# A hybrid of two network blocks on one core: two heads in turn in the state-space loop, the rotary steps behind it, and other places for units of the first block

## The chip, the core and the metric

The kernel is one program on one core of a Trainium2 chip. The metric is the device time in microseconds of one execution, and the median of the runs is compared. Five engines run side by side, each through its own list of instructions: TensorE (PE) multiplies matrices into PSUM, VectorE (DVE) and ScalarE (ACT) read and write PSUM and SBUF, GpSimd (POOL) does some small work, and SyncE (SP) issues the transfers of weights. They wait for each other through semaphores.

## What is computed

256 tokens of width 1024 go through a first block (a mixer of two kinds of attention, and experts) and then twice through a second block (feed-forward, mixer, feed-forward). All of it is fp32.

```python
def first_block(x, ...):
    u = rmsnorm(h, norm_mix_g) @ w_in
    o_sb = stick_breaking(u[..., :1536])           # 8 heads of 64, softplus of the scores, suffix sums
    o_rw = rwkv7(u[..., 1536:])                    # 8 heads of 64: S_t = S_{t-1} diag(w_t) + (S_{t-1} (-kk_t)) (kk_t * a_t)^T + v_t k_t^T
    h = h + concat([o_sb, o_rw]) @ w_out
    return rmsnorm(h + experts(rmsnorm(h)))        # 32 experts, 2 of them weighted per token

# in rwkv7, the norms of the keys:
    kk = k * k_k
    kk = kk * rsqrt(max(sum(kk * kk, over a head), 1e-24))

def second_block(x, ...):
    for l in range(2):
        x = x + 0.5 * swiglu(rms_norm(x), ...)
        u = rms_norm(x) @ w_in[l]
        y_ssd  = ssd_mixer(...)     # state space, 16 heads of 64, both directions, chunks of 128
        y_mla  = mla_mixer(...)     # 8 heads, 64 + 32 rotary, softmax
        y_conv = conv_mixer(...)    # depthwise, 3 taps
        x = x + concat([y_ssd, y_mla, y_conv]) @ w_out[l]
        x = x + 0.5 * swiglu(rms_norm(x), ...)

def ssd_chunked(x, dt, a, bm, cm):  # one direction
    decay  = exp(where(lower, a_cs[l] - a_cs[s], -inf))
    cb     = einsum('lgn,sgn->lsg', cm, bm)
    y_diag = einsum('lsg,lsgr,sgrp->lgrp', cb, decay, x * dt)
    y_off  = cm @ (state of the chunk before) * exp(a_cs)
    return y_diag + y_off
```

## The kernel before

**Layout.** Activations stand as feature x token in tiles of 128 partitions x 256 tokens. The token dimension is two chunks of 128 (`tok(0)`, `tok(1)`), and a 64-wide head fills one half of the partitions, so a tile `f` holds two heads, 2f and 2f + 1. The working memory is one arena addressed; PSUM is eight banks `PS[0]` to `PS[7]` of 128 x 512 elements. `bank(b, mark)` on PE waits until the work that `mark` names has read bank b, and notes who will empty it next.

**fp32 products.** The projections and the feed-forward split each operand into a high part and a rest, and add three products (`mm3`). The weights come through a ring of five slots of 128 x 2048 elements. SP fills a slot when PE is through with the load five before (`spent`), ACT makes the high part (`rhi`, line 2260), DVE the rest (`rlo`, line 1486), and PE waits for both in `take(n)`. In SSD, in the attentions and in the key norms the operands are plain fp32 or exact constants and are multiplied once (`mm`).

**Order of work.** No planner stands between the source and the engines. Each engine has a function (tensor, vector, scalar, gpsimd, sync) in which its steps are called in the order in which it runs them, and semaphores join the engines: `hit` marks a step, `wait_ge` waits for one. Where a helper records an operation, all of its uses have one line: 538 a matmul, 541 a transpose, 1475 a scalar_tensor_tensor, 1478 a tensor_scalar, 2260 an activation.

**First block.** Its units are the rw projections j = 0 to 6 (PE), each with a weight pass of DVE (`ahead`) and DVE's shift mixing; the sums of squares of the keys and their spread over a head (`head_sums`, `head_spread`, `kk`; reciprocal in line 1565); `decays`, `inputs` and `kk_a` on DVE; the attention matrices of four groups g and their masks (line 1697 and the ones near it); the first level of a block inverse (`level_first`, with transposes, and the copy of line 1576); six projections `sb_proj(i)` in the banks of `sb_bank`; the bonus term (line 1708); and `inverse`, whose units u step through levels and groups, `level_y(u)` and `level_x(u)`, DVE's part being line 1611 and, for the last level, line 1613. Stick-breaking softplus, weights, values and sums are hung onto units u by number in the lists of PE, DVE and ACT.

**State-space loop.** For each k = 2h + d (head h, direction d) PE builds the exponent of the decay in bank k % 4 (`ssd_decay`), ACT takes its exponential into one of `NM` buffers `Md`, in two halves with their own bias, and DVE multiplies it by `cb` (line 2154). `ssd_values(h)` multiplies it with the inputs `xd`: four matmuls of 128 x 64 on 128 tokens, into the lower or upper 64 partitions of bank 4 + f % 4. For an odd head it then adds the far terms of both directions with two matmuls on the identity, and DVE adds the skip term (line 1475). Before the loop's values stand the states and `ssd_far`. `head_rope(1, step)` is DVE's share of the query and key norms and the rotation of the second half of the tokens, called from within this loop at k = 9, 17 and 25 (lines 2062 to 2079).

**Heads behind it.** `turn_heads(tt)` transposes queries and keys, `conv_tile` is a half tile of projection (24 matmuls) for the third mixer, and then for h = 0 to 8 a half tile, `scores(h + 1)`, `turned(h)` and `values(h - 1)` follow each other. DVE takes the maximum of the scores (line 2168), ACT the exponential, PE transposes it, DVE copies it out of PSUM (line 2175), PE multiplies it with the values. Between them ACT and DVE make the parts of the next weights, the first of them in `mixer_load`.

Of the kernel before, what the change touches and what calls it, by code (L numbers as in the profile page):

```python
# [170 lines left out]
def program(nc, I, out):  # L171

    MUL, ADD, SUB, MAX, EQ = ALU.mult, ALU.add, ALU.subtract, ALU.max, ALU.is_equal
    with ExitStack() as ctx:
# [215 lines left out]
        sb_bank = lambda i: (4, 6, 5, 7, 3, 2)[i]  # L390
# [64 lines left out]
        NM = 6  # L455
        Md = v3(B0 + 9264, NM)
# [64 lines left out]
        def tensor(e, w):  # L521
# [246 lines left out]
            def inverse():  # L768

                for u in range(4, NU + 2):  # L770
                    if u < NU:
                        level_y(u)
                    if u in (6, 7, 15, 16):
                        h = {6: 0, 7: 2, 15: 4, 16: 6}[u]
                        sb_weights(h)
                        sb_weights(h + 1)
# [3 lines left out]
                    if u in (18, 19):  # L780
                        sb_values(u - 16)
                    if 20 <= u < 26:
                        masked((u - 20) // 3, (u - 20) % 3)
                    if u == 21:
                        w.wait_ge("sb_sq")
                        head_sums(sq2, 3, "sb")
                    if u in (24, 26):
                        spread_half(3, "sb", u // 26, ("sb_m", u // 26 * 2 + 1))
# [131 lines left out]
            def first_block():  # L920
                w.dma(d_first, 32)
                norm(0)
                for j, f in enumerate(RW_F):
# [40 lines left out]
                sb_scores(1)  # L964
                sb_proj(5)
# [237 lines left out]
            def mixer(l):  # L1203
# [116 lines left out]
                def ssd_values(h):  # L1320
                    po, f, ob = 64 * (h % 2), h // 2, 4 + (h // 2) % 4
                    if po == 0:
                        bank(ob, ("yo", l, f))
                    for d in range(2):
                        w.wait_ge("md", l, 2 * h + d)
                        for c in range(2):
                            w.wait_ge("xd", l, 2 * c + 1)
                            p = mm(PS[ob][po:po + 64, tok(c)], xd[d][:, c, h * 64:h * 64 + 64], Md[:, (2 * h + d) % NM, tok(c)], d + c == 0, d + c == 2)
                    if po:
                        for d in range(2):  # L1330
                            w.wait_ge("far", l, d, f // 4)
                            p = mm(PS[ob][:, tok(1 - d)], y_far[d][:, 128 * f:128 * f + 128], C("ident"), False, d == 1)
                    p.then_inc(*w.hit("yv", l, h))
# [1646 lines left out]
```

## Time and profile before

| what | value |
|---|---|
| runs | 1900.99, 1900.48, 1890.29 us, median 1900.48 |
| profiled execution | 1892.44 us, its span 1890.7 us |
| PE, DVE, ACT busy | 1819.9, 1202.1, 941.8 us |
| state-space loop, layer 0 | 928.71 to 959.31 us |
| scores of head 0 to values of head 7, layer 0 | 971.50 to 1023.11 us |
| first block up to the inverse | 0 to 119.46 us |

The profile's page gives busy time by engine and a row for each group of instructions. The timeline lists what an engine does in the order of time: the start in us from the span's start, the duration of the group, the engine and line, what is written and read, partitions and shapes, the count, and in brackets the idle time ahead of it and who ended it. The profile records an fp32 matmul as two, so a count of 8 stands for four matmuls. Rows of PE overlap a little, since the matmuls are pipelined; from start to start is the safe way to read what a step costs.

### The profile page before, as it was taken

What the parts mean: (1) busy time and instruction counts of PE and PEld (TensorE: products, weight loads), DVE (VectorE), ACT (ScalarE), POOL (GpSimd) and SP (SyncE); (2) the same over time, 40 slices, a digit from 0 to 9 for tenths busy, and PEclk for the clock granted to TensorE, in tenths of its full rate; (3) what the DMA queues carried; (4) which work ended last, traced back from release to release, by engine and by line L of the source; (5) the groups of instructions that cost most, each with busy time, mean ns of one, the idle gap of its engine ahead of it and who ended that gap; (6) DMA issues with size and microseconds to landing.
All of it is one profiled execution on the core that took longest, in us unless ns stands there. A gap on an engine that the chain in (4) does not pass through costs nothing.

```text
span 1890.7 us, 26150 instructions
## 1 busy us (share of the span) xinstructions
PE 1819.9 (96%) x10830; PEld 1579.7 (84%) x10830; DVE 1202.1 (64%) x1510; ACT 941.8 (50%) x1231; POOL 104.3 (6%) x78
## 2 busy tenths in 40 slices
PE   7899989999999899989999999999998999999999
PEld 7888788888888788878898888888887988888887
DVE  5945568677777855448857655455555696756553
ACT  6444356455654644347554454444434666445442
POOL 1413011000000000000110000000000012000000
PEclk9999989999999999999999999999999999999999
DMA  8320146899999455545222465556654541245653
GB/s 275 113 71 1 34 157 223 303 343 333 338 333 324 142 178 189 190 134 178 90 68 91 155 200 179 192 168 197 190 189 145 168 134 35 100 157 182 193 180 111
DMA packets 191063, 329.93 MB, mean 175 GB/s; under 512 B 7776, under 2 KB 150496, under 8 KB 186592
## 3 DMA queue, kind: packets, MB, share of 16 engines
q1 hardware_dynamic: 190800, 327.74, 52.3%
q8 instruction: 85, 1.39, 0.3%
q0 software_dynamic: 144, 0.52, 0.1%
q14 instruction: 34, 0.28, 0.0%
HBM read 327.18 MB, written 1.05 MB: 174 GB/s over the span
## 4 chain that ended last, share of the span: by engine, by line
PE 78%; DVE 12%; ACT 4%; DMA 3%; issue 2%; POOL 1%; SPq 0%; DVEq 0%; ACTq 0%; POOLq 0%
PE ps L538 75%; DVE rlo L1486 3%; PE ps L541 3%; DVE arena L1475 2%; ACT rhi L2260 2%; DMA ring<-in_exp_w_up 2%; ACT arena L2260 1%; DMA ring<-in_w_in 1%; DVE xnl L1475 1%; DVE arena L1478 1%; DVE small L2168 0%; DVE xtok L1475 0%; POOL arena L2823 0%; DVE small L2055 0%; DVE arena L2198 0%
## 5 line engine op out<-in xcount | busy, mean ns | idle before, releaser
L1486 DVE TENSOR_TENSOR rlo<-ring,rhi 128x2048 fp32r<-128x2048 f32 x274 | 627.0, 2290 | 372.5 <-ACT rhi L2260 372.1
L2260 ACT ACTIVATE rhi<-ring 128x2048 fp32r<-128x2048 f32 x274 | 521.4, 1906 | 281.0 <-PE ps L538 134.2
L538 PE MATMUL ps<-rhi,xnh 128*128 128x512 f32 (+1 forms) x768 | 301.8, 393 | 0.8 <-DVE arena L1708 0.8
L538 PE MATMUL ps<-rhi,xnl 128*128 128x512 f32 (+1 forms) x768 | 296.4, 386 | 0.0
L538 PE MATMUL ps<-rlo,xnh 128*128 128x512 f32 (+1 forms) x768 | 296.0, 385 | 0.0
L538 PE MATMUL ps<-xnh,rhi 128*128 128x256 f32 (+2 forms) x824 | 242.9, 295 | 3.0 <-DVE xnl L1475 3.0
L538 PE MATMUL ps<-xnl,rhi 128*128 128x256 f32 (+2 forms) x824 | 236.6, 287 | 0.0
L538 PE MATMUL ps<-xnh,rlo 128*128 128x256 f32 (+2 forms) x824 | 236.4, 287 | 0.0
L538 PE MATMUL ps<-rhi,hhi 128*128 128x512 f32 x544 | 205.4, 395 | 0.0
L538 PE MATMUL ps<-rhi,xwr 128*128 128x512 f32 x528 | 180.5, 404 | 2.2 <-issue 1.9
L538 PE MATMUL ps<-arena 128*128 128x128 f32 (+10 forms) x1256 | 165.1, 297 | 16.3 <-DVE arena L2175 9.4
L2260 ACT ACTIVATE arena<-ps 128x512 f32<-128x512 f32 (+4 forms) x196 | 93.8, 497 | 163.2 <-PE ps L538 97.0
L538 PE MATMUL ps<-rhi,hlo 128*128 128x512 f32 x448 | 172.2, 390 | 2.2 <-DVE hlo L2228 2.2
L538 PEld LDWEIGHTS ps<-rhi,xnh 128*128 128x128 f32 x768 | 144.4, 188 | 31.1 <-DVE arena L1708 1.6
L538 PE MATMUL ps<-rlo,hhi 128*128 128x512 f32 x432 | 169.1, 391 | 0.0
L538 PEld LDWEIGHTS ps<-rhi,xnl 128*128 128x128 f32 x768 | 144.3, 188 | 29.5
L538 PEld LDWEIGHTS ps<-rlo,xnh 128*128 128x128 f32 x768 | 144.6, 188 | 27.7 <-issue 0.5
L538 PEld LDWEIGHTS ps<-xnh,rhi 128*128 128x128 f32 (+2 forms) x824 | 159.9, 194 | 6.7 <-issue 6.1
L538 PEld LDWEIGHTS ps<-arena 128*128 128x128 f32 (+3 forms) x1256 | 132.1, 175 | 36.5 <-DVE arena L2175 11.0
L538 PEld LDWEIGHTS ps<-xnl,rhi 128*128 128x128 f32 (+2 forms) x824 | 159.9, 194 | 1.3 <-issue 1.0
L538 PEld LDWEIGHTS ps<-xnh,rlo 128*128 128x128 f32 (+2 forms) x824 | 159.4, 193 | 0.3
L538 PEld LDWEIGHTS ps<-arena,ring 128*128 128x128 f32 x1056 | 124.0, 194 | 7.0 <-issue 5.0
(237 smaller groups left out, 2204.7 us busy)
## 6 DMA issues: line engine op xcount, KB each, us to landing
ring<-in_w_in SPq DMA_DIRECT2D x47, 1024.0 KB, 5.4
ring<-in_ffn_w_gate SPq DMA_DIRECT2D x88, 512.0 KB, 4.0
ring<-in_ffn_w_up SPq DMA_DIRECT2D x88, 512.0 KB, 5.0
ring<-in_ffn_w_down SPq DMA_DIRECT2D x44, 1024.0 KB, 4.9
ring<-in_exp_w_down SPq DMA_DIRECT2D x35, 1024.0 KB, 5.6
ring<-in_exp_w_gate SPq DMA_DIRECT2D x66, 512.0 KB, 4.2
ring<-in_exp_w_up SPq DMA_DIRECT2D x66, 512.0 KB, 5.5
ring<-in_w_out SPq DMA_DIRECT2D x20, 1024.0 KB, 4.9
```

Of the source, the lines that this page charges most:

```text
L538: return e.matmul(o, lhsT, rhs, start=start, stop=stop, skip_group_check=True)
L541: return e.transpose(o, x, C("ident")[0:x.shape[0], 0:x.shape[0]])
L1475: return e.scalar_tensor_tensor(out=o, in0=a, scalar=s, in1=b, op0=op0, op1=op1)
L1478: return e.tensor_scalar(o, a, s1, None, op0) if s2 is None else e.tensor_scalar(o, a, s1, s2, op0, op1)
L1486: e.tensor_tensor(lo, raw, f32(hi), SUB).then_inc(*w.hit("lo", n))
L2260: return e.activation(o, x, func, **kw)
```

## The change

In the state-space loop a step is now a tile f, with both of its heads:

- `ssd_values(f)` waits for all four `Md` of the tile, and then issues eight value matmuls in a row, writing the lower and the upper 64 partitions of the bank by turns, and then the far terms. Four decay exponents stand in a row ahead of it.
- `NM` is 8 instead of 6; the last two buffers lie elsewhere in the arena.
- DVE's three rotary steps and ACT's and DVE's part of weight tile 14 stand behind the loop (ACT's did before).
- One half tile `conv_tile` moves from behind head 7's turn (h = 8) to a place ahead of `turn_heads(1)`.

In the first block:

- The spread of the key norms (`head_spread`, "kk") goes behind projection 5 on PE; DVE sums the key squares in `decays`, and runs `inputs` behind the weight pass of projection 5 rather than behind the mixing of projection 4. The masks of `at` wait for `kT` as well.
- `sb_proj(1)` goes ahead of `level_first(2)` and `level_first(3)`; `sb_proj(4)` uses bank 1, not 3.
- `level_y(4)` goes ahead of `sb_proj(5)` on PE and DVE.
- Softplus, weights, values and the sums of the second half of the sb heads come one unit later; `sb_m` on DVE stands behind the x step of its unit.

```diff
-        sb_bank = lambda i: (4, 6, 5, 7, 3, 2)[i]
+        sb_bank = lambda i: (4, 6, 5, 7, 1, 2)[i]
...
-        NM = 6
-        Md = v3(B0 + 9264, NM)
+        NM = 8
+        Md = [ar(B0 + 9264 + 256 * i, 256) for i in range(6)] + [ar(9480 + 256 * i, 256) for i in range(2)]
...
-                    if u < NU:
+                    if 4 < u < NU:
                         level_y(u)
-                    if u in (6, 7, 15, 16):
-                        h = {6: 0, 7: 2, 15: 4, 16: 6}[u]
+                    if u in (6, 7, 16, 17):
+                        h = {6: 0, 7: 2, 16: 4, 17: 6}[u]
                         sb_weights(h)
...
                         head_sums(sqk, 2, "kk")
-                    if j == 4:
+                    if j == 5:
                         head_spread((1, 2), "kk", (("kk", 0), ("kk", 1)))
-                    if j == 5:
...
+                sb_proj(1)
                 level_first(2)
                 level_first(3)
-                sb_proj(1)
...
+                level_y(4)
                 sb_proj(5)
                 inverse()
...
-                def ssd_values(h):
-                    po, f, ob = 64 * (h % 2), h // 2, 4 + (h // 2) % 4
-                    if po == 0:
-                        bank(ob, ("yo", l, f))
+                def ssd_values(f):
+
+                    ob = 4 + f % 4
+                    bank(ob, ("yo", l, f))
+                    w.wait_ge("xd", l, 3)
+                    for h in (2 * f, 2 * f + 1):
+                        for d in range(2):
+                            w.wait_ge("md", l, 2 * h + d)
                     for d in range(2):
-                        w.wait_ge("md", l, 2 * h + d)
                         for c in range(2):
-                            w.wait_ge("xd", l, 2 * c + 1)
-                            p = mm(PS[ob][po:po + 64, tok(c)], xd[d][:, c, h * 64:h * 64 + 64], Md[:, (2 * h + d) % NM, tok(c)], d + c == 0, d + c == 2)
-                    if po:
-                        for d in range(2):
-                            w.wait_ge("far", l, d, f // 4)
-                            p = mm(PS[ob][:, tok(1 - d)], y_far[d][:, 128 * f:128 * f + 128], C("ident"), False, d == 1)
-                    p.then_inc(*w.hit("yv", l, h))
+                            for h in (2 * f, 2 * f + 1):
+                                po = 64 * (h % 2)
+                                mm(PS[ob][po:po + 64, tok(c)], xd[d][:, c, h * 64:h * 64 + 64], Md[(2 * h + d) % NM][:, tok(c)], d + c == 0, d + c == 2)
+                    for d in range(2):
+                        w.wait_ge("far", l, d, f // 4)
+                        p = mm(PS[ob][:, tok(1 - d)], y_far[d][:, 128 * f:128 * f + 128], C("ident"), False, d == 1)
+                    p.then_inc(*w.hit("yv", l, f))
...
-                for k in range(4, 36):
-                    if k < 32:
-                        ssd_decay(k)
-                    if k % 2 == 0:
-                        ssd_values((k - 4) // 2)
+                for f in range(8):
+                    if f < 7:
+                        for k in range(4 * f + 4, 4 * f + 8):
+                            ssd_decay(k)
+                    ssd_values(f)
...
                 conv_tile(*halves_.pop(0))
                 turn_heads(0)
                 conv_tile(*halves_.pop(0))
+                conv_tile(*halves_.pop(0))
                 turn_heads(1)
...
                 for h in range(9):
-                    conv_tile(*halves_.pop(0))
+                    if h < 8:
+                        conv_tile(*halves_.pop(0))
...
-                    if u in (4, 5, 13, 14):
-                        h = {4: 0, 5: 2, 13: 4, 14: 6}[u]
+                    if u in (4, 5, 14, 15):
+                        h = {4: 0, 5: 2, 14: 4, 15: 6}[u]
                         sb_softplus(h)
...
-                    if u in (25, 27):
-                        half = u // 27
-                        w.wait_ge("hr_spread", "sb", half)
...
+                    if u in (26, 28):
+                        half = u // 28
+                        w.wait_ge("hr_spread", "sb", half)
...
+                head_sums(2, 1e-24, None, MAX, None, "kk")
                 own(p)
...
             def kk_a():
-                head_sums(2, 1e-24, None, MAX, None, "kk")
...
+                    if j == 5:
+                        inputs()
...
-                    if j == 4:
-                        inputs()
...
                 ahead(ld("sb", 4))
+                level_y(4)
                 ahead(ld("sb", 5))
...
-                        e.tensor_tensor(Md[:, k % NM], Md[:, k % NM], cb[:, k // 16], MUL).then_inc(*w.hit("md", l, k))
+                        e.tensor_tensor(Md[k % NM], Md[k % NM], cb[:, k // 16], MUL).then_inc(*w.hit("md", l, k))
...
-                    if k in (9, 17, 25):
-                        head_rope(1, (k - 9) // 8)
-                    if k == 32:
-                        part(mixer_load(l, 14))
+                for step in range(3):
+                    head_rope(1, step)
+                part(mixer_load(l, 14))
```

PE at the start of the state-space loop; `ps0` to `ps3` are the banks of the decay exponents, `ps4` that of the values of the first tile. Before:

```order
L538 MATMUL ps0<-cst_r 128x256
L538 MATMUL ps4<-arena 64x128 x4
L538 MATMUL ps1<-yr,cst_r 128x256
L538 MATMUL ps1<-cst_r 128x256
L538 MATMUL ps2<-yr,cst_r 128x256
L538 MATMUL ps2<-cst_r 128x256
L538 MATMUL ps4<-arena 64x128 x4
L538 MATMUL ps4<-cst,arena 128x128 x2
```

The same place now:

```order
L538 MATMUL ps0<-cst_r 128x256
L538 MATMUL ps1<-yr,cst_r 128x256
L538 MATMUL ps1<-cst_r 128x256
L538 MATMUL ps2<-yr,cst_r 128x256
L538 MATMUL ps2<-cst_r 128x256
L538 MATMUL ps3<-yr,cst_r 128x256
L538 MATMUL ps3<-cst_r 128x256
L538 MATMUL ps4<-arena 64x128 x8
L538 MATMUL ps4<-cst,arena 128x128 x2
```

The two groups of four value matmuls, with two decays between them, are one group of eight behind four decays.

DVE in the last third of the same loop. `rlo` is the weight pass, the rows on `rope` and `row` are rotary steps. Before:

```order
L1475 SCALAR_TENSOR_TENSOR arena<-arena,prm,ps 128x256
L2154 TENSOR_TENSOR arena<-arena 128x256
L2074 TENSOR_TENSOR arena<-arena,rope 128x256
L2075 TENSOR_TENSOR arena<-arena,rope 128x256
L2076 TENSOR_TENSOR arena<-arena,rope 128x256
L2077 TENSOR_TENSOR arena<-arena,rope 128x256
L2078 TENSOR_TENSOR arena<-arena 128x16x16
L2079 TENSOR_TENSOR arena<-arena 128x16x16
L2154 TENSOR_TENSOR arena<-arena 128x256 x3
```

Now, behind the last products:

```order
L2165 TENSOR_TENSOR arena<-arena 128x256 x3
L1480 SCALAR_TENSOR_TENSOR arena<-arena,prm,ps 128x256 x2
L2073 RECIPROCAL small<-small 128x16
L2074 TENSOR_TENSOR arena<-arena,small 128x1536
L2079 TENSOR_TENSOR arena<-arena,row 128x1536
L2085 TENSOR_TENSOR arena<-arena,rope 128x256
L2086 TENSOR_TENSOR arena<-arena,rope 128x256
L2087 TENSOR_TENSOR arena<-arena,rope 128x256
L2088 TENSOR_TENSOR arena<-arena,rope 128x256
L2089 TENSOR_TENSOR arena<-arena 128x16x16
L2090 TENSOR_TENSOR arena<-arena 128x16x16
L1491 TENSOR_TENSOR rlo<-ring,rhi 128x2048
```

The nine rotary instructions have left the loop, and the weight pass that closed the loop comes behind them.

DVE in the first block, around `inputs` (the rows on 128x4x128, and 1655 and 1657 ahead of them). Before:

```order
L1486 TENSOR_TENSOR rlo<-ring,rhi 128x2048
L1475 SCALAR_TENSOR_TENSOR arena<-arena,prm 128x256 x2
L1655 TENSOR_TENSOR arena<-arena,ps 128x512 x2
L1657 TENSOR_TENSOR arena<-arena 128x1024
L1475 SCALAR_TENSOR_TENSOR arena<-arena 128x4x128
L1663 TENSOR_TENSOR arena<-arena 128x4x128
L1664 TENSOR_TENSOR arena<-arena 128x4x128
```

Now:

```order
L1491 TENSOR_TENSOR rlo<-ring,rhi 128x2048
L1480 SCALAR_TENSOR_TENSOR arena<-arena,prm 128x256 x2
L1491 TENSOR_TENSOR rlo<-ring,rhi 128x2048
L1664 TENSOR_TENSOR arena<-arena,ps 128x512 x2
L1666 TENSOR_TENSOR arena<-arena 128x1024
L1480 SCALAR_TENSOR_TENSOR arena<-arena 128x4x128
L1672 TENSOR_TENSOR arena<-arena 128x4x128
L1673 TENSOR_TENSOR arena<-arena 128x4x128
```

One more weight pass stands ahead of `inputs`, and it is followed by the mixing of projection 5 instead of by the pass.

## Rows read from the trace of the kernel before

**Rows 1.** The page, part 1: busy us, share of the span, instructions.

```profile
PE 1819.9 (96%) x10830; PEld 1579.7 (84%) x10830; DVE 1202.1 (64%) x1510; ACT 941.8 (50%) x1231; POOL 104.3 (6%) x78
```

**Rows 2.** Timeline of PE, state-space loop of layer 0: start, duration, group, idle ahead.

```profile
928.71 0.68 PE L538 MATMUL ps<-yr,cst_r 128*128 128x256 f32 x1
...
944.59 0.71 PE L538 MATMUL ps<-cst,arena 128*128 128x128 f32 x4
945.06 0.37 PE L538 MATMUL ps<-yr,cst_r 128*128 128x256 f32 x1
...
946.73 0.38 PE L538 MATMUL ps<-yr,cst_r 128*128 128x256 f32 x1
...
947.39 1.09 PE L538 MATMUL ps<-arena 128*64 128x128 f32 x8
948.40 0.71 PE L538 MATMUL ps<-cst,arena 128*128 128x128 f32 x4
...
959.31 0.36 PE L538 MATMUL ps<-xnh,rhi 128*128 128x256 f32 x1
...
962.26 1.91 PE L541 MATMUL ps<-cst,arena 128*96 128x128 f32 x16
```

**Rows 3.** Timeline of ACT, same loop: exponentials of the decays.

```profile
926.85 2.17 ACT L2260 ACTIVATE arena<-ps,arena 128x128 f32<-128x128 f32 x8
...
947.26 1.14 ACT L2260 ACTIVATE arena<-ps,arena 128x128 f32<-128x128 f32 x4 [0.54 <-PE ps L538]
```

**Rows 4.** Timeline of DVE, same loop and what follows it.

```profile
929.92 1.75 DVE L2154 TENSOR_TENSOR arena<-arena 128x256 f32<-128x256 f32 x5
...
937.41 1.76 DVE L2063 TENSOR_TENSOR arena<-arena,small 128x1536 f32<-128x1536 f32 x1
...
952.39 0.41 DVE L2074 TENSOR_TENSOR arena<-arena,rope 128x256 f32<-128x256 f32 x1
...
972.63 0.69 DVE L2168 TENSOR_REDUCE small<-ps 128x2 f32<-128x512 f32 x1 [10.34 <-PE ps L538]
```

**Rows 5.** Timeline of PE, heads: scores of head 0, values of head 7 (layers 0, 1).

```profile
971.50 1.02 PE L538 MATMUL ps<-arena 128*128 128x256 f32 x4
...
1023.11 1.97 PE L538 MATMUL ps<-arena 128*128 128x64 f32 x8 [2.70 <-DVE arena L2175]
...
1648.22 1.10 PE L538 MATMUL ps<-arena 128*128 128x64 f32 x8 [2.68 <-DVE arena L2175]
```

**Rows 6.** Timeline of DVE, end of the heads of layer 0: a weight pass.

```profile
1016.70 2.29 DVE L1486 TENSOR_TENSOR rlo<-ring,rhi 128x2048 fp32r<-128x2048 f32 x1 [2.30 <-ACT rhi L2260]
```

**Rows 7.** Timeline of PE, first block: matmuls of 64 columns, halves by turns.

```profile
196.38 1.09 PE L538 MATMUL ps<-cst,small 128*64 128x128 f32 x16 [0.36 <-DVE arena L1475]
...
202.87 1.09 PE L538 MATMUL ps<-xnl_free,arena 128*64 128x128 f32 x16
```

**Rows 8.** Windows behind head 7, layers 0 and 1: length, busy, granted clock, DMA.

```profile
1023.10:1029.40 6.30, 6.29 (x19) 5.33 (x20) 6.05 (x9) 0.00 (x0) 0.00 (x0) 0.50 0.26 107
1648.20:1654.40 6.20, 6.18 (x31) 5.28 (x32) 5.95 (x9) 0.00 (x0) 0.00 (x0) 1.00 0.25 100
```

**Rows 9.** Timeline of PE, first block: spread of key norms, first level's transposes.

```profile
53.90 3.69 PE L538 MATMUL ps<-cst,small 128*64 128x128 f32 x32 [3.47 <-DVE small L1565]
...
85.62 1.91 PE L541 MATMUL ps<-cst,arena 128*128 128x128 f32 x16
```

**Rows 10.** Waits of PE, 80 to 300 us: us in total, times, longest.

```profile
PE ps L538 <- DVE arena L1611: 1.8, 1, 1.8
PE ps L541 <- DVE arena L1576: 1.6, 2, 1.0
PE ps L538 <- DVE arena L1613: 1.3, 2, 1.1
...
PE ps L538 <- DVE arena L1708: 0.8, 1, 0.8
```

**Rows 11.** Timeline of DVE, first block: the four masks.

```profile
83.21 2.47 DVE L1697 TENSOR_TENSOR arena<-ps,cst 128x512 f32<-128x512 f32 x4
```

More of the change, by code:

```diff
@@ L779, in inverse @@
                         sb_scores(u - 7)
[L780 to L781 removed]
+                    if u in (19, 20):
+                        sb_values(u - 17)
                     if 20 <= u < 26:
                         masked((u - 20) // 3, (u - 20) % 3)
[L784 removed]
+                    if u == 22:
                         w.wait_ge("sb_sq")
                         head_sums(sq2, 3, "sb")
[L787 to L788 removed]
+                    if u in (25, 27):
+                        spread_half(3, "sb", u // 27, ("sb_m", u // 27 * 2 + 1))
                     if 4 <= u - 1 < NU:
@@ L1578, in level_first, with level_y @@
                 e.tensor_tensor(XT[g], Y[:, gs], wide("ident"), ADD).then_inc(*w.hit("x", 0, g))
+            def level_y(u):
+                li, g = units[u]
+                gs = slice(4 * g, 4 * g + 4)
+                w.wait_ge("ly", u)
+                if li < LAST:
+                    e.tensor_copy(Y[:, gs], four(0)).then_inc(*w.hit("y", u))
+                else:
+                    e.tensor_copy(Y[64:128, gs, 0:64], four(0)[64:128, :, 0:64]).then_inc(*w.hit("y", u))
             def inverse():
@@ L1582, in inverse @@
                     if u < NU:
-                        li, g = units[u]
-                        gs = slice(4 * g, 4 * g + 4)
-                        w.wait_ge("ly", u)
-                        if li < LAST:
-                            e.tensor_copy(Y[:, gs], four(0)).then_inc(*w.hit("y", u))
-                        else:
-                            e.tensor_copy(Y[64:128, gs, 0:64], four(0)[64:128, :, 0:64]).then_inc(*w.hit("y", u))
-                    if u in (4, 5, 13, 14):
-                        h = {4: 0, 5: 2, 13: 4, 14: 6}[u]
+                        if u > 4:
+                            level_y(u)
+                    if u in (4, 5, 14, 15):
+                        h = {4: 0, 5: 2, 14: 4, 15: 6}[u]
                         sb_softplus(h)
@@ L1595, in inverse @@
                         masked((u - 20) // 3, (u - 20) % 3)
-                    if u == 22:
+                    if u == 23:
                         head_sums(3, 1.0 / 64, 1e-6, MUL, ADD, "sb")
-                    if u == 23:
+                    if u == 24:
                         head_rec("sb")
-                    if u in (25, 27):
-                        half = u // 27
-                        w.wait_ge("hr_spread", "sb", half)
-                        for f in (2 * half, 2 * half + 1):
-                            stt(sbo[:, f], sbo[:, f], pr("sb_out_g", f), PS[3][:, 256 * (f % 2):256 * (f % 2) + 256], MUL, MUL).then_inc(*w.hit("sb_m", f))
                     if u > 4:
@@ L1613, in inverse @@
                             e.tensor_tensor(XT[g][0:64, :, 64:128], four(1)[0:64, :, 0:64], XT[g][0:64, :, 64:128], ADD).then_inc(*w.hit("x", li, g))
+                    if u in (26, 28):
+                        half = u // 28
+                        w.wait_ge("hr_spread", "sb", half)
+                        for f in (2 * half, 2 * half + 1):
+                            stt(sbo[:, f], sbo[:, f], pr("sb_out_g", f), PS[3][:, 256 * (f % 2):256 * (f % 2) + 256], MUL, MUL).then_inc(*w.hit("sb_m", f))
             def masked(c, k):
```

15 lines of the change are left out of this document (8 added, 7 removed).

## Prediction

> **What bounds the kernel now.** I read the page first: TensorE (PE) is busy for 1819.9 of 1890.7 us, VectorE (DVE) for 64% and ScalarE (ACT) for 50% [rows 1]. The other engines matter only where they make PE wait, and a change can win in two ways: fewer microseconds of PE work, or fewer waits. So I then read PE's timeline stage by stage, noting from start to start what each stage costs and which gaps it holds.
>
> The state-space loop of layer 0 runs from 928.71 to 959.31, 30.6 us, and layer 1 has the same. One f (two heads) takes 3.81 us, 944.59 to 948.40: far terms to 945.06 (0.47), then twice four decay matmuls (946.73 to 947.39, 0.66) and the values of one head (to 948.40, 1.01) [rows 2]. The profile records an fp32 matmul twice, so a head's four value matmuls are 8 records, at 127 ns. PE has next to no gap, so what the loop costs is PE work. ACT issues its exponentials every 0.26 us (8 in 2.17, the last one lasting 0.37) and waits 0.54 or more for PE before a batch of four [rows 3]. DVE's decay products are issued every 0.33 us (5 in 1.75, the last lasting 0.43), and its rotary steps stand between them: two of about 1.75 us, six of 0.41 and a small one, 6.0 us in all; behind the loop it idles for 10.34 us [rows 4].
>
> The attention heads behind it are bounded by something else. From scores of head 0 (971.50) to the values of head 7 (1023.11) are 51.6 us, and the last step waits 2.70 us for DVE's copy of line 2175, in layer 1 2.68 us [rows 5]. DVE is there because it waited 2.30 us for ACT's copy of a weight tile before its own pass over that tile [rows 6], and ACT's copy stood behind an exponential that needs DVE's maximum: DVE and ACT turn each other, and PE follows.
>
> **The loop, two heads in turn.** Removed: nothing of PE's arithmetic. The 8 value matmuls of an f are issued in a row and write the lower and upper 64 partitions of the bank by turns. The nearest rows are exactly that form: 16 records of 128 rows x 64 columns and 128 elements take 1.09 us, in different banks at 202.87 and within one bank at 196.38 [rows 7]; 8 records in one half take the same 1.09 us [rows 2]. So 64 ns against 127. Per f: far 0.47, values 1.02, decays 8 x 0.117 + 0.2 for going in and out of the half-width form (four now take 0.66, so 0.19 of it is that) = 1.14; together 2.63 against 3.81. At the start values(0) now needs four decay products and not two: two more at 0.33, so it starts about 931.1 where it started at 930.5. Then 1.02 + 0.47, six periods of 2.63, 0.2 of wait for the last products (the last group has no decays to cover them) and 1.49: end at 950.1. **Gain 9.2 us a layer, 18.4 in all.** The floor from ACT is 8 x 0.26 = 2.1 us an f, from DVE 4 x 0.33 + 0.4 = 1.7, with the two extra buffers giving exponentials one f of lead; both lie under 2.63, but ACT by 0.5 only. Bounds: no overlap of the halves gives 0.2 an f, all overlap as above.
>
> The Trainium skill, "TensorEngine Tiling (Array Packing)", section "PSUM Bottleneck", warns that tiling speeds TensorE and not the reading of PSUM, which may become the limit. By that rule the loop would run at ACT's pace; that is a rival below.
>
> **Rotary steps behind the loop** (about 6.0 us of DVE). They fall into the 10.34 us idle [rows 4]: last product 950.5, rotary done about 957, the weight pass to 959.3. Their consumer, the second turn of the heads, comes after three half tiles of projection and one turn: 950.1 + 3 x 2.95 + 1.67 = 960.6 (a half tile is 959.31 to 962.26 [rows 2]). Cost nothing, with 3.6 us to spare.
>
> **One half tile of projection moved** from behind head 7's turn to before the second turn of the heads. Its 2.95 us of PE work now lie before scores(0). The 51.6 us after scores(0) are set by the DVE and ACT chain, which starts with scores(0) and holds no less work than before. So head 7's values still come 51.6 us after scores(0), and the wait there grows from 2.70 to 5.65 us: the tile was free cover and is now on the path. **Cost 2.95 a layer, 5.9.** Bounds: 0 if the chain got shorter by as much, 5.9. I take the upper end, since no row shows that chain waiting for a tile that moves.
>
> **Clock.** After the 2.70 us wait of layer 0 PE ran at half the clock (1.2 GHz), 0.50 granted for 6.3 us and 19 records; after the 2.68 us of layer 1 at 1.00, with 31 records in 6.2 [rows 8]. A fall costs 6.3 x 12/31 = 2.4 us. With 5.65 us of idle I expect it in both layers, part of it inside the idle: **cost 2.0**, bounds 0 and 4.8.
>
> The Trainium skill, "TensorE: Matmul & The Clock Gate", section "HAM oscillation", says that idle gaps between bursts of matmuls drop the clock, each time anew; by it layer 1 pays a whole fall, 2.4. By rows alone, one of two such waits paid.
>
> **First block.** (a) The spread of the key norms goes from behind projection 4 to behind projection 5. It waited 3.47 us, and its 32 records took 3.69 us where 2.1 is usual [rows 7, 9]: the clock had fallen there too, 2.4 at the price above. A projection of 5.9 us (two half tiles) covers the wait: 5.9 gained at once. DVE's sum moves ahead of its differences, so ACT's exponentials start some 2 us sooner. But `inputs` (DVE, about 7 us) now follows the weight pass of the next tile, and DVE's masks had no slack at all: they ended at 85.68 [rows 11], when PE came at 85.62 [rows 9]. They come earlier by only 2.3 to 5, so PE waits there 1 to 2.7; I take 1.8. (b) sb_proj(1) ahead of the transposes of groups 2 and 3 covers their two waits, 1.6. (c) Another bank for sb_proj(4) removes the 0.8 for line 1708 [rows 10]. Sum of (a) to (c): 5.9 + 1.6 + 0.8 - 1.8 = 6.5, bounds 5 and 8.8. (d) level_y(4) earlier: 0.2 only, since the step after it needs DVE, which then waits for ACT's logarithms. (e) softplus a step later cuts the wait of 1.8 for line 1611 to about 0.3, gain 1.5; sb_m behind the x step takes most of the 1.3 for line 1613 [rows 10], gain 1.0. **First block 9.2**, bounds 6 and 12.
>
> **Sum.** 18.4 + 9.2 - 5.9 - 2.0 = 19.7 us off the profiled execution: 1892.4 to 1872.7. The median of the runs shown (1900.5) stands 8 above the profiled one; the four values lie in two groups, 1890.3 and 1892.4, 1900.5 and 1901.0. I can't tell which the changed kernel falls into, so I add half the distance, 4: **1877 us**. About 1%, or 19 us, is what a measurement can tell from no change. The rivals' times below have the 4 in them.
>
> **Rivals.**
> - The tile is not on the path after all and no clock is lost: 7.9 more, 1869. For: a chain of DVE and ACT may shorten when its PE inputs come early. Against: at 1016.70 it waited for ACT, not for PE [rows 6]. Chance 0.12.
> - ACT sets the loop's pace. Two batches of four with the waits seen between (0.54 each) make 2 x (1.14 + 0.35) = 3.0 us, not 2.63: six periods x 0.37 x 2 layers = 4.4 less gain, 1881. For: 0.5 us of margin. Against: waits of ACT in [rows 3] are for PE. Chance 0.13.
> - DVE holds the first block: the spread's gain is given back at the masks, 4 in place of 9.2, 1882. Chance 0.17.
> - Slower: within one bank, accumulating matmuls of the two halves don't overlap, and each change of half costs the 0.1 us that entering the half-width form costs now. An f is then 16 x 0.127 + 8 x 0.1 = 2.83 for the values, 0.8 more; 16 f make 12.8, less 3.0 for fewer form changes, plus 1.3 at the starts: 11.1 slower, with the rest (9.2 - 7.9) 9.8 slower than before: 1902 against the profiled 1892, 1906 with the 4. It decides from 141 ns a record. Against: the row at 196.38, though that one does not accumulate. Chance 0.05.
> - The pairing saves the form changes (3.0) and costs the starts (1.3), nothing else: 1.7, and with the rest (9.2 - 7.9 = 1.3) 3.0 in all, 1893. Chance 0.03.
> - The forecast, 1877 with its own range 1869 to 1885: 0.50.
>
> **Numbers.** Range 1864 to 1889: below it lies little of the first rival, above it the last two and part of the third. Faster by over 1% (under 1881.5) takes the first rival, most of the forecast and a third of the next two, less what the two groups of runs blur: 0.55. Within 1%: 0.42. Slower by over 1%: 0.03.
>
> **What would show it.** The loop's first decay to first projection in 21 to 22 us; 16 value records in 1.09; ACT waiting for PE in each batch; DVE's rotary steps in one piece behind the loop; scores(0) to the values of head 7 again 51.6 us, with a wait near 5.6; the granted clock 0.5 after it in both layers; no gap before the key spread and none at group 2's transposes, a new one of 1 to 3 us before group 0's. It is wrong if the wait at head 7 stays at 2.7, if value records take over 100 ns, or if PE waits for the decay products each f.

## The result, and the profile after

The changed kernel takes 1885.04 us (median of 13 runs, 1882.02 to 1888.73), the kernel before 1896.15 in 13 runs (1890.29 to 1903.13). The ratio is 0.9944, interval 0.9928 to 0.9959: about 10.6 us faster (11.1 by the medians). The forecast of 1877 was for a gain of 20 us, profile against profile; the profiled executions are 10.4 apart (spans 1890.7 and 1880.3).

Part 1 of the page of the changed kernel:

```profile
PE 1805.8 (96%) x10830; PEld 1571.4 (84%) x10830; DVE 1202.7 (64%) x1510; ACT 940.2 (50%) x1231; POOL 103.6 (6%) x78
```

14.1 us less of PE work than in [rows 1], on a span that is 10.4 shorter: some of what was saved came back as waiting. Timeline of PE, state-space loop of layer 0, changed kernel:

```profile
926.88 0.68 PE L538 MATMUL ps<-yr,cst_r 128*128 128x256 f32 x1
...
929.67 1.09 PE L538 MATMUL ps<-arena 128*64 128x128 f32 x16 [1.29 <-DVE arena L2165]
...
931.16 0.36 PE L538 MATMUL ps<-yr,cst_r 128*128 128x256 f32 x1
...
932.27 1.09 PE L538 MATMUL ps<-arena 128*64 128x128 f32 x16
...
945.30 1.09 PE L538 MATMUL ps<-arena 128*64 128x128 f32 x16
...
947.87 1.09 PE L538 MATMUL ps<-arena 128*64 128x128 f32 x16 [0.83 <-DVE arena L2165]
...
949.36 0.36 PE L538 MATMUL ps<-xnh,rhi 128*128 128x256 f32 x1
```

From values to values it is 2.60 us (929.67 to 932.27) where [rows 2] gave 3.81, and the 16 value records take 1.09. The loop lasts 22.5 us, 926.88 to 949.36, not 30.6. ACT and DVE of the same loop, two fences:

```profile
944.71 2.17 ACT L2270 ACTIVATE arena<-ps,arena 128x128 f32<-128x128 f32 x8 [0.43 <-PE ps L538]
```

```profile
949.64 0.48 DVE L1480 SCALAR_TENSOR_TENSOR arena<-arena,prm,ps 128x256 f32<-128x256 f32 x1 [1.53 <-PE ps L538]
...
956.64 2.29 DVE L1491 TENSOR_TENSOR rlo<-ring,rhi 128x2048 fp32r<-128x2048 f32 x1
...
965.57 0.69 DVE L2178 TENSOR_REDUCE small<-ps 128x2 f32<-128x512 f32 x1 [6.61 <-PE ps L538]
```

ACT waits 0.43 for PE in a tile, so it doesn't set the pace; the rotary steps fill the stretch from 950.0 to 956.6, and 6.61 of idle is left of the 10.34 in [rows 4]. Timeline of PE, the heads (both layers):

```profile
964.44 1.02 PE L538 MATMUL ps<-arena 128*128 128x256 f32 x4
...
1016.04 1.97 PE L538 MATMUL ps<-arena 128*128 128x64 f32 x8 [5.61 <-DVE arena L2185]
...
1636.04 1.97 PE L538 MATMUL ps<-arena 128*128 128x64 f32 x8 [5.61 <-DVE arena L2185]
```

Scores of head 0 to the values of head 7 last 51.6 us as in [rows 5], and the wait has gone from 2.70 to 5.61. The windows behind it, which answer to [rows 8], layer 1 first. A row of this view gives the window and its length, then for PE, PE's weight loads, DVE, ACT and POOL the busy us and in brackets the number of records, then the granted clock, the DMA share and GB/s:

```profile
1636.00:1642.20 6.20, 6.16 (x22) 5.30 (x23) 5.95 (x9) 0.00 (x0) 0.00 (x0) 0.64 0.00 0
1016.00:1022.30 6.30, 6.26 (x19) 5.29 (x20) 6.05 (x9) 0.00 (x0) 0.00 (x0) 0.50 0.01 3
```

Layer 1, which kept its clock before (31 records), now has 22 records in 6.2 us. Timeline of PE, first block of the changed kernel: the spread of the key norms, then three waits:

```profile
56.10 1.97 PE L538 MATMUL ps<-cst,small 128*64 128x128 f32 x32
...
75.40 0.39 PE L538 MATMUL ps<-xnh,rhi 128*128 128x256 f32 x1 [1.93 <-DVE rlo L1491]
...
118.32 2.05 PE L538 MATMUL ps<-arena 128*128 128x128 f32 x8 [2.48 <-DVE arena L1590]
...
196.10 3.27 PE L538 MATMUL ps<-arena,xnh_free 128*128 128x64 f32 x16 [1.29 <-DVE arena L1480]
```

The first product behind the inverse starts at 196.10; before it was at 200.94. From there to the first matmul of the output projection, in the kernel before:

```profile
200.94:209.62 8.68, 8.68 (x115) 8.20 (x113) 2.41 (x6) 2.48 (x5) 0.00 (x0) 1.00 0.01 2
```

and in the changed kernel:

```profile
196.10:211.11 15.01, 15.01 (x112) 14.28 (x112) 2.03 (x5) 2.58 (x5) 0.00 (x0) 0.55 0.01 1
```

The same work takes 15.0 us at a granted clock of 0.55 instead of 8.7 at 1.00. Here the first block's lead of 4.8 us is lost, with 1.5 more. PE was not idle for long before the fall: it shows waits of 0.32, 0.49, 0.60 and 1.29 us between 190 and 196, and was busy for 3.40 of these 6.0 us. In the kernel before, the six us ahead of the same product are these:

```profile
194.94:200.94 6.00, 4.31 (x60) 3.53 (x59) 4.18 (x11) 0.60 (x1) 0.00 (x0) 1.00 0.01 3
```

It waited there too, 0.36, 0.22 and 1.11 us, and was busy for 4.31. Taking the start of a DVE weight pass as the milestone, the changed kernel is 1.5 us behind at 233 us, 0.3 ahead when the experts are done, 7.0 ahead behind layer 0's mixer and 10.4 behind layer 1's.

### The profile page after: what moved, and what is told of

Its sections match the earlier page's. It is cut to its first block, busy times and chain, and to the rows that moved or that the text cites. A ratio compares the mean times of both kernels' runs of the same rounds, so it can differ in the third digit from the quotient of the medians.

```text
span 1880.3 us, 26177 instructions
## 1 busy us (share of the span) xinstructions
PE 1805.8 (96%) x10830; PEld 1571.4 (84%) x10830; DVE 1202.7 (64%) x1510; ACT 940.2 (50%) x1231; POOL 103.6 (6%) x78
## 4 chain that ended last, share of the span: by engine, by line
PE 78%; DVE 14%; ACT 4%; DMA 2%; issue 1%; POOL 0%; SPq 0%; DVEq 0%; ACTq 0%
PE ps L538 75%; DVE rlo L1491 4%; PE ps L541 3%; DVE arena L1480 3%; ACT rhi L2270 2%; ACT arena L2270 1%; DMA ring<-in_exp_w_up 1%; DMA ring<-in_w_in 1%; DVE xnl L1480 1%; DVE arena L1483 1%; DVE arena L2120 1%; DVE small L2178 0%; DVE xtok L1480 0%; DVE small L2066 0%; DVE arena L2165 0%
## 5 line engine op out<-in xcount | busy, mean ns | idle before, releaser
L538 PE MATMUL ps<-arena 128*128 128x128 f32 (+10 forms) x1256 | 153.2, 303 | 23.1 <-DVE arena L2185 15.2
L538 PEld LDWEIGHTS ps<-arena 128*128 128x128 f32 (+3 forms) x1256 | 124.4, 181 | 40.5 <-DVE arena L2185 16.7
```

The costliest lines, as they stand in the source:

```text
L538: return e.matmul(o, lhsT, rhs, start=start, stop=stop, skip_group_check=True)
```

## The experiments

All ratios are to the kernel before in the same runs; 0.001 is 1.9 us. A difference between two experiments is that of their ratios. Where the two intervals overlap, the times alone don't separate the two kernels, and the text says so.

**Second block alone.** The kernel before with `ssd_values(f)`, `NM = 8`, the rotary steps and the half tile as in the change:

```diff
 (first block as before)
-                for k in range(4, 36):
+                for f in range(8):
...
+                conv_tile(*halves_.pop(0))
                 turn_heads(1)
```

> The kernel before with the second block's part of the change alone (two heads in turn, 8 buffers, rotary steps behind the loop, the half tile ahead of the second turn of the heads). My theory from the two traces: this part is worth 10 us (6.7 in layer 0, 3.5 in layer 1, where a clock fall of 6.8 us is new), the first block's part nothing. So 1880.5 profiled against 1890.7, a ratio of 0.9947 to the kernel before. Rival: the parts share the gain as the forecast had it, in proportion 10.5 to 9.2; then this kernel has about half of the measured 11 us, a ratio of 0.997.

Measured 1889.57 us, 0.9965 (0.9946 to 0.9984). By the ratio 6.6 us; the rival's 0.997 is in the interval, and so, at its very edge, is my 0.9947. Its trace settles more than its time. From 900 us on it gains 9.9 us on the profile of before, as the changed kernel does (10.2). But up to 900 us it is the same program as the kernel before, and it is 8 us later at 233. Its window from the first product behind the inverse to 218.40:

```profile
202.71:218.40 15.69, 15.69 (x117) 14.51 (x115) 2.50 (x6) 3.53 (x7) 0.00 (x0) 0.56 0.00 1
```

So the fall of the clock in this place belongs to the kernel before as well. The one execution profiled there had escaped it. The six us ahead of the product in this run:

```profile
196.71:202.71 6.00, 4.32 (x60) 3.53 (x59) 4.18 (x11) 0.60 (x1) 0.00 (x0) 1.00 0.01 3
```

They are those of the kernel before to within 0.01 us. The same instructions with the same idling kept the clock in one execution and lost it in the other; what decides between the two no run here shows.

**First block alone.**

```diff
 (second block as before)
-                    if j == 4:
+                    if j == 5:
                         head_spread((1, 2), "kk", (("kk", 0), ("kk", 1)))
...
+                sb_proj(1)
                 level_first(2)
```

> The kernel before with the first block's part of the change alone. My theory from the traces: the weights of the first mixer's output come 4.8 us earlier at 196 us, then TensorE's clock falls to 0.5 for over 10 us and takes it all back; the experts start within 2 us of where they did, and what is left there is absorbed by the experts' transfers. Ratio 1.000, between 0.999 and 1.001, and the granted clock 0.5 somewhere between 190 and 215 us. Rival, the forecast's: 9.2 us faster, ratio 0.995. Second rival: the fall is an accident of where this profile fell; then the median is 3 to 5 us faster, 0.998.

Measured 1892.48, 0.998 (0.9965 to 0.9995), the second rival's figure; the clock did fall at 197 us. In its profile the block gains nothing. The median gains, probably since the kernel before mostly pays for that fall too.

**Half tile back behind head 7's turn**, all else as changed:

```diff
-                conv_tile(*halves_.pop(0))
                 conv_tile(*halves_.pop(0))
                 turn_heads(1)
...
-                    if h < 8:
-                        conv_tile(*halves_.pop(0))
+                    conv_tile(*halves_.pop(0))
```

> The changed kernel with the half tile of projection back behind head 7's turn. My theory: the heads' chain of DVE and ACT lasts 51.6 us from scores(0) wherever the tile is, the rotary steps are done at 956.6 and the second turn of the heads comes at 956.9, so scores(0) start 2.95 us earlier and the wait at head 7 is 2.7 again: 5.9 us less than the changed kernel, ratio to before 0.991. With the shorter wait layer 1 may also keep its clock (another 2). Rival: the rotary steps or ACT's copies of the first turn hold the second turn, and the tile was no loss: the same time as the changed kernel, 0.9944.

Measured 1875.63, 0.9902 (0.9878 to 0.9925), 8 us below the changed kernel's ratio and faster than both kernels. Its PE timeline at the values of head 7:

```profile
1012.26 1.10 PE L538 MATMUL ps<-arena 128*128 128x64 f32 x8 [2.69 <-DVE arena L2183]
```

5.61 is 2.69 again. The tile costs the 5.9 that were forecast, plus some 2 for clock: behind this shorter wait layer 0 kept it, while layer 1 lost it here too:

```profile
1626.08 1.97 PE L538 MATMUL ps<-arena 128*128 128x64 f32 x8 [2.70 <-DVE arena L2183]
```

These eight records take 1.10 at full clock and 1.97 at half.

**Heads one after the other** within the eight value matmuls:

```diff
-                        for c in range(2):
-                            for h in (2 * f, 2 * f + 1):
+                    for h in (2 * f, 2 * f + 1):
+                        for d in range(2):
+                            for c in range(2):
```

> The changed kernel with the eight value matmuls of a tile in the order head by head, not by turns; all else equal. My theory: the gain of the loop is that matmuls into the two halves of the partitions overlap when they follow each other. Then 16 value records take 2.03 us and not 1.02, the period of a tile 3.6 and not 2.61, and the kernel is 16 x 1.0 = 16 us slower than the changed kernel, ratio to before 1.003. Rival: what counts is that the eight stand in a row behind four decays; then 2.6 stays and the ratio is 0.9944.

Measured 1889.81, 0.9978 (0.9963 to 0.9994): 6.4 us slower than the changed kernel, between my 16 and the rival's nothing. Two tiles in its PE timeline:

```profile
941.53 1.58 PE L538 MATMUL ps<-arena 128*64 128x128 f32 x16
...
944.62 1.58 PE L538 MATMUL ps<-arena 128*64 128x128 f32 x16
```

The overlap of the halves is real, and my size for its loss was wrong: 16 records take 1.5 us, not 2.03, and a tile 3.09, not 3.6. In the records those of one half start 0.110 us apart, and the first of the second head starts 0.49 us behind the first of the first, with three of the first head's still to come. Even in blocks of eight some of it overlaps. Turns give 0.49 us a tile over blocks (7.8 us in 16), blocks 0.7 over the kernel before.

**The later sb units undone** (softplus, weights, values, sums, sb_m as before):

```diff
-                    if u in (6, 7, 16, 17):
+                    if u in (6, 7, 15, 16):
...
-                    if u in (26, 28):
+                    if u in (25, 27):
```

> The changed kernel with the softplus, weights, values, sums and sb_m units of the second half of the sb heads where they were before, all else as changed. My theory: the later units put sb_m's second half behind the last x step, so that the first product behind the inverse waits 1.29 us for its bank; with the gaps of 0.3 to 0.6 ahead of it TensorE is busy for 2.2 of 4 us there, and its clock falls for 13.65 us, at a price of 6.8. With the units back the waits are those of before, the fall comes in some executions only (as in the profile of the second block's part alone, and not in that of the kernel before), and the wait of 1.5 for the softplus steps returns: 1 to 5 us faster than the changed kernel, ratio to before 0.9925. Rival: the fall has nothing to do with these units; then 1.5 to 2.5 us slower, 0.9955.

Measured 1881.69, 0.9929 (0.9914 to 0.9944). That overlaps with the changed kernel's interval, so it is unclear whether these edits cost anything in all. In this profile the first product behind the inverse starts at 199.1, 3 us later than in the changed kernel (six profiles with the changed kernel's first block have it between 194.3 and 196.7), and the clock fell to half for 13.65 us from 200.6. The units don't cause the fall.

**Idle matmuls in the last level**, on the kernel with the tile back:

```diff
+                    if u in (27, 28):
+                        filler(3)
                     if 4 <= u - 1 < NU:
                         level_x(u - 1)
...
                 inverse()
+                filler(5)
                 rhs_values(0)
```

> The kernel with the tile back, and eleven matmuls of constants (128x128, their result is never read) in the last level of the inverse: three ahead of each of the last two x steps, five ahead of the first product behind it. They compute nothing. My theory: TensorE's clock falls there because it idles; with work in the gaps it stays at full clock, 13.65 us of half clock become 6.8, and at most 1 us of the filler is not inside a gap: 6 us faster than the kernel with the tile back, ratio to before 0.987. Rival: the fall comes from the half-height matmuls or from the stages ahead, and the filler costs its 0.5 to 2.4 us: 0.991.

Measured 1872.71, 0.9876 (0.9859 to 0.9893): 5 us less than with the tile back, though the two intervals overlap. Its windows, the last level with the filler, then the same work as in the windows above:

```profile
192.45:197.77 5.32, 5.32 (x55) 4.61 (x55) 2.01 (x5) 0.02 (x1) 0.00 (x0) 1.00 0.00 0
197.77:206.44 8.67, 8.67 (x113) 8.19 (x112) 1.99 (x5) 2.57 (x5) 0.00 (x0) 1.00 0.01 2
```

8.67 at full clock against 15.0: the fall costs 6.3 us. The filler itself costs 1.1 (5.32 against 4.23 without it). The rival, that the half-height matmuls or the stages ahead bring the fall, is out, since the filler leaves both as they were. Over all the profiles of these experiments, the fall stands in this place in eight of the nine kernels without a filler (the one that escaped is the kernel before) and in none of the five with it. PE's idling is what makes the fall possible.

The Trainium skill, "TensorE: Matmul & The Clock Gate", section "HAM oscillation", describes a kernel whose clock falls anew at each idle gap between bursts of matmuls. The trace agrees that the fall follows idling, but no single gap here was above 1.3 us, less than the gaps of that kernel.

**Rotary steps back within the loop**, on the kernel with the tile back:

```diff
-                for step in range(3):
-                    head_rope(1, step)
...
+                    if k in (9, 17, 25):
+                        head_rope(1, (k - 9) // 8)
```

> The kernel with the tile back, and the three rotary steps again within the state-space loop (behind products 9, 17 and 25), everything else equal. My theory: in the paired loop DVE has 0.25 us to spare in a tile of 2.6, so the 6.3 us of rotary steps push TensorE: the loop grows by about 4.5 us a layer, less the time by which the second turn no longer waits (nothing): 9 us slower than with the tile back, ratio 0.995. Rival: the eight buffers give DVE enough lead, and the loop grows by under 1 us a layer: 0.991.

Measured 1891.38, 0.9977 (0.9964 to 0.999), 14 us slower than with the tile back. PE in its loop:

```profile
939.48 1.09 PE L538 MATMUL ps<-arena 128*64 128x128 f32 x16 [1.68 <-DVE arena L2163]
...
946.44 1.09 PE L538 MATMUL ps<-arena 128*64 128x128 f32 x16 [1.69 <-DVE arena L2163]
...
953.86 1.09 PE L538 MATMUL ps<-arena 128*64 128x128 f32 x16 [2.14 <-DVE arena L2163]
```

5.5 us of waits a layer, all for DVE's products, and the clock fell at 955. I had expected 9; the direction and the place are as said. With the steps left inside the loop the pairing would have given back most of its gain.

**DVE's copy of head 7 first**, on the kernel with the tile back:

```diff
                     if h == 6:
+                        turned(7)
                         gated(1)
                         gated_conv((0, 1))
```

> The kernel with the tile back, and DVE's copy of head 7's turned weights ahead of its two conv steps (gated(1), gated_conv of tiles 0 and 1, 3.5 us) instead of behind them. My theory: the wait of 2.7 us at the values of head 7 is DVE's order, not the length of the chain: the copy is done at 1008.7, the tile's matmuls end at 1009.6, no wait is left in either layer, and the clock does not fall there: 5.4 us of waits and 1 to 3 us of clock, ratio to before 0.987. Rival: the conv steps come late in turn and the head sums of the conv part, or the next weight pass, wait for them by as much: 0.990.

Measured 1872.5, 0.9878 (0.9864 to 0.9892). The next row of PE behind the values of head 7:

```profile
1017.18 0.47 PE L538 MATMUL ps<-rhi,hhi 128*128 128x512 f32 x1 [1.75 <-ACT arena L2269]
```

The wait of 2.69 was DVE's order, and it is gone; 1.75 came in its place, for ACT's copy of the last conv tile, which stands behind a weight pass. A second wait grew as well, 1.23 us for DVE's reciprocal of the conv norms (0.20 and none with the tile back). In the profile the waits of a layer thus add up to as much as without this edit; what is gone is the fall of the clock behind head 7 in layer 1. The ratio is 0.0024 lower, 4.6 us, with intervals that overlap.

**All of it together**: tile back, copy first, filler, and ACT's copy ahead of its weight pass:

```diff
+                    if h == 8:
+                        cbg_of(1)
                     if h in (0, 2, 4, 6, 8):
                         part(mixer_load(l, 16 + h // 2))
```

> The kernel with the tile back and DVE's copy of head 7 first, and with two more edits: ACT copies the last conv tile out of PSUM ahead of its weight pass, and the eleven idle matmuls stand in the last level of the inverse. My theory: the wait of 1.75 us that took the place of head 7's goes, 3.5 us in two layers, and the fall of the clock at 196 goes, 5: ratio to before 0.983, no gap over 0.8 us at the start of the output projection. Rival: the next weight pass comes late by as much, and only the filler's 5 is left: 0.985.

Measured 1871.8, 0.9882 (0.9858 to 0.9906), where 0.983 was expected: by the ratio no better than the filler or the copy alone. It has the lowest median, by 0.7 us, which is no difference. PE's next wait:

```profile
1030.92 1.39 PE L538 MATMUL ps<-cst,small 128*64 128x128 f32 x16 [3.09 <-DVE small L1576]
```

Head 7's wait is gone from both layers, and 3.09 us stand in each layer's output projection, where DVE's reciprocal for the conv norms is behind a weight pass. With the tile back the waits from head 7's values to these norms add up to 2.7 to 2.9 us a layer, with the copy first to 2.98, here to 3.09: the chain of DVE and ACT decides, and its end has only moved.

**The filler in three more kernels**: before, changed, and the first block alone. The edit is the same.

> The kernel before with the same eleven idle matmuls in the last level of the inverse. My theory: the fall of the clock there comes in most executions of the kernel before too (its profile is one of the fastest of them, and the second block's part alone, the same program up to that point, showed it), so the filler makes its median 3 to 5 us faster: ratio 0.998. Rival: the first block's part of the change brought the fall, and the filler costs the kernel before 1 to 2 us: 1.001.

> The changed kernel with the same eleven idle matmuls. My theory: 5 us less than the changed kernel, ratio to before 0.9915. Against the kernel before with the filler this gives the change without that fall: 13 to 15 us by the traces (4.8 of the first block, 5.2 a layer of the second, less clock). Rival: the first block's 4.8 us are lost again in the experts, whose weights arrive at the pace of the transfers: 10 us.

> The first block's part of the change alone, with the same eleven idle matmuls. My theory: against the kernel before with the filler it has what the first block's part is worth at full clock, 4 to 5 us and not the forecast's 9.2: ratio to before 0.9955. Rival: the experts give the 4.8 back, 0.998.

Measured 1890.54, 0.9981 (0.9966 to 0.9997); 1880.58, 0.9925 (0.9901 to 0.9949); 1887.17, 0.9959 (0.9946 to 0.9973). The kernel before gains some 4 us (0.6 to 6.4 by the interval) from matmuls that compute nothing. The fall costs 6.3 and the filler 1.1, so most of its executions seem to pay for the fall. With that cost out of both, the first block's part is worth 0.0022 or 4 us (the first product behind the inverse starts at 197.57 against 202.30, 4.7 earlier), and the whole change 0.0056 or 10.6 us: the rival's 10, not my 13 to 15. That leaves 6.4 for the second block, as its own kernel gave. By the intervals each of these differences is uncertain by 4 to 5 us.

In the profile of the changed kernel with the filler the experts gave 6.5 us back; with the first block alone, the same program up to there, none. PE in the window 300 to 600 us of the first, and two waits of ACT in 300 to 620:

```profile
300.00:600.00 300.00, 292.33 (x1787) 256.71 (x1787) 224.03 (x187) 163.93 (x155) 0.96 (x1) 0.99 0.91 320
```

```profile
ACT rhi L2278 <- DMA ring<-in_exp_w_up: 132.1, 62, 5.6
ACT arena L2278 <- PE ps L541: 12.5, 4, 5.4
```

and of the second:

```profile
300.00:600.00 300.00, 294.72 (x1808) 261.02 (x1806) 227.62 (x190) 166.32 (x157) 2.68 (x1) 0.99 0.93 326
```

```profile
ACT rhi L2274 <- DMA ring<-in_exp_w_up: 127.3, 62, 5.9
```

ACT waits 4.8 us longer for weights in the first, at 320 against 326 GB/s. Counting matmul records, the first goes from 1.7 us ahead of the second at 300 us to 3.1 behind it at 600, and loses 2.4 more by 665, where its clock fell to half for 6.8 us at 625 and the other's did not. So the experts' length differs between executions by about as much as the first block gains, in part by the pace of the weights and in part by the clock.

## Why the prediction was right, and where it was not

The range held 1885, the sign was right, and the gain was forecast at nearly twice what came. That the range held it owes much to its width, 1864 to 1889: the outcome that had the best chance, faster by over 1% (0.55), did not come. By its steps, profile against profile:

- **Loop, 9.2 a layer: 8.1.** The tile was forecast at 2.63 and took 2.60. The two ends were too cheap: 2.79 us from the first decay to the first values where 2.4 was in the sum, and 2.57 from the values of the last tile but one to those of the last where 1.7 was, both waits for DVE's products (1.29 and 0.83).
- **Rotary steps at nothing:** right. They end at 956.6, ahead of 957 as forecast, and the experiment that puts them back shows the cover was needed.
- **Half tile 5.9:** right, 51.6 us again and 5.61 against 5.65, and undone it gives this back, with 2 for clock. But my reason, that the chain can't be shortened there, was too strong: DVE's order held the last copy, and with the copy first the wait went elsewhere.
- **Clock behind head 7, 2.0:** right in the profile, both layers fell, and layer 1 lost 1.8 that it had not lost before. The other profiles bear it out: with a wait of 5.61 the values of head 7 ran at half clock in all ten cases of five profiles, with one of 2.7 the clock fell at them or within 2 us behind them in nine cases of fourteen.
- **Second block in all:** 10.2 in these two profiles, 10.5 in the forecast, but 6.4 to 6.6 by the ratios. The near match was in part luck: from the end of the experts to the end, four profiles whose second block is that of the kernel before take 1052.0 to 1055.8 us, and the one I had was among the slow ones (1055.6; it shows a fall of the clock at 900 us that two of the others don't). Four with the second block as changed take 1045.3 to 1047.9. The means are 7.8 apart.
- **First block, 9.2: this step failed.** The forecast of each part stands in brackets; the sizes are read from the two profiles at equal numbers of matmul records, and of the parts only (e) was undone by itself. (a) gave 6.3 at the spread (5.9) and lost 2.5 at the attention products and the masks (1.8), for `inputs`. (b) gave 1.5 (1.6), (c) 1.1 (0.8). Then (d) cost 2.5 where 0.2 was to be won: PE waits 2.48 at 118.32 for the copy of the next y step, where it had waited 0.88 and 0.48, and DVE stands there behind a softplus step that waited 3.12 us for ACT; behind the wait the clock was at half for 3.4 us. (e) gave 0.8 (2.5): the wait of 1.8 for line 1611 is gone, but in the last level PE now waits 2.70 us in all, not 1.69. (With (e) undone this place comes 3 us later in the profile, 1.7 of it by one more fall of the clock, for 3.4 us at 149.) It makes 4.8 at 196 us. There the clock fell for 13.65 us, at 6.3, and this was in no term. So in the profile nothing was left of the 9.2, and with the filler, which takes the fall out of both kernels, 4. I had looked for falls of the clock in the profile of before, found full clock in this place, and read that as a property of the kernel. It was one lucky execution of it.
- **The 4 us for two groups of runs:** with 13 runs, at 1890.3, 1893.7 to 1896.9 and 1900.0 to 1903.1, two groups are not to be told. The profiled execution was 3.7 below the median; the fall that it lacks is worth 6.3. The changed kernel's median is 3.0 above its own profiled execution, though that one has the fall, so the 4 came near for no reason of the forecast's.

Of the rivals, DVE holding the first block (1882) comes nearest in time, in part by its mechanism: 2.5 us were lost at the masks, but 2.5 more at the y step and all of the rest to the clock. ACT did not set the loop's pace: it waits 0.43 us for PE in each tile. By the rule of the Trainium skill, "TensorEngine Tiling (Array Packing)", section "PSUM Bottleneck", the reading of PSUM might have become the limit; these waits show that it had not yet.

## What to carry to other kernels

A profile is one execution: where the engine's gaps are short and many, compare two profiles of the same program before counting on its clock, and price a stage at both. Matmuls into the two halves of the partitions cost half here when they followed each other by turns (16 records in 1.02 us, where 8 in one half took the same); what stands between them on the other engines has then to be moved out, or it becomes the wait. A piece of independent PE work behind a chain of other engines is cover: moved ahead of the chain's first step, it was on the path at its full length (2.95 us a layer).

## What was not expected of the hardware

- Gaps of 0.3 to 1.3 us, no more, were followed by 13.65 us at half clock, a price of 6.3 us; eleven matmuls of constants kept the clock in all five kernels that had them. Up to that place the same instructions, with the same 1.7 us of waits in 6, fell in one profile and not in another.
- Value records of one half start every 0.110 us whether or not the other half is busy, and eight in one half followed by eight in the other overlap by themselves for three records: 1.5 us, between 1.02 by turns and the 2.03 that the rows of before suggested.
